# Matmuls of ones with the identity, read by nobody, ahead of thirteen steps of TensorE in the first two blocks

## The reference

```
first block:   h = rms_norm(x); proj = h @ w_in
               differential attention (4 heads x 2 maps) and block attention (8 heads), partial rope, gated by silu
               x = x + (sigmoid(g_a) * y_a + sigmoid(g_b) * y_b) @ w_out
               x = x + sigmoid(x @ w_ple_gate) * (p @ w_ple);  x = rms_norm(x)
second block:  mod = silu(c) @ w_mod + b_mod      (six vectors of 1024)
               h = rmsnorm(x) * (1 + sc1) + sh1;  proj = h @ w_in_2
               attention over compressed keys, selected blocks and a window, with a relative bias; short convolution
               x = x + gt1 * (concat(rmsnorm(o_attn), rmsnorm(o_conv)) @ w_out_2)
               h2 = rmsnorm(x) * (1 + sc2) + sh2
               x = x + gt2 * peer(h2)             (8 heads pick 16 of 16384 experts each)
out = rmsnorm(x)
```

## Time and profile before

| | |
|---|---|
| median of 3 runs | 1353.32 us (1350.22 to 1356.21) |
| profiled execution, its own time | 1355.46 us |
| its span, first to last instruction | 1353.7 us |
| mean granted clock of TensorE | 0.968 |
| TensorE matmul busy | 1251.1 us (92% of the span) |
| TensorE weight load busy | 1145.1 us (85%) |
| VectorE busy | 850.4 us (63%) |
| ScalarE busy | 711.5 us (53%) |
| POOL busy | 582.5 us (43%) |
| chain that ended last | PE 50%, POOL 21%, issue 14%, DVE 8%, ACT 4%, DMA 2% |

### The profile page before, as it was taken

The page is one execution under the profiler, slowest core; times in us unless marked ns, Lnnn a source line. Parts: engine busy times, 40 slices in busy tenths (PEclk is TensorE's granted clock), DMA queues, the critical chain, the costliest instruction groups (busy, mean ns, idle before and its releaser), DMA issues.

```text
span 1353.7 us, 26683 instructions
## 1 busy us (share of the span) xinstructions
PE 1251.1 (92%) x8546; PEld 1145.1 (85%) x8546; DVE 850.4 (63%) x1810; ACT 711.5 (53%) x1473; POOL 582.5 (43%) x500
## 2 busy tenths in 40 slices
PE   7979989977889888989899999999999999999996
PEld 6968878875877688989899999999978878888885
DVE  4596767877445553999645555553067767676765
ACT  5435757434545544645564444445555655555554
POOL 2563454432326632899986666667800000000000
PEclk8999999988899898999999999999999999999998
DMA  6575645674543333445455655565567675756552
GB/s 217 163 237 166 221 169 193 206 237 136 191 164 128 126 114 121 156 155 186 140 171 179 188 178 188 178 188 181 193 233 250 200 246 189 255 195 249 195 191 93
DMA packets 85471, 249.35 MB, mean 184 GB/s; under 512 B 7931, under 2 KB 29563, under 8 KB 84508
## 3 DMA queue, kind: packets, MB, share of 16 engines
q1 hardware_dynamic: 77212, 209.69, 47.0%
q0 software_dynamic: 8192, 38.80, 8.2%
HBM read 235.36 MB, written 13.11 MB: 184 GB/s over the span
## 4 chain that ended last, share of the span: by engine, by line
PE 50%; POOL 21%; issue 14%; DVE 8%; ACT 4%; DMA 2%; POOLq 1%; DVEq 0%; ACTq 0%; SPq 0%
PE psum L625 49%; POOL w_lo L1382 19%; DVE s_sb L1512 2%; POOL arena L1448 2%; DMA arena<-mods 1%; ACT w_hi L1048 1%; DVE w_lo L1503 1%; PE psum L788 1%; ACT arena L1185 1%; DVE arena L1732 1%; DMA s_sb<-routing_weights 1%; DVE rstd L1497 1%; POOLq L1381 0%; DVE arena L1618 0%; DMA par<-params 0%
## 5 line engine op out<-in xcount | busy, mean ns | idle before, releaser
L1048 ACT ACTIVATE w_hi<-ring 128x512 fp32r<-128x512 f32 x734 | 452.3, 629 | 416.2 <-PE psum L625 408.5
L1382 POOL TENSOR_TENSOR w_lo<-ring,w_hi 128x512 fp32r<-128x512 f32 x367 | 502.2, 1376 | 299.3 <-ACT w_hi L1048 292.1
L625 PE MATMUL psum<-h_hi,w_hi 128*128 128x256 f32 x1832 | 541.2, 295 | 53.3 <-DVE w_lo L1503 16.5
L625 PE MATMUL psum<-h_lo,w_hi 128*128 128x256 f32 x1832 | 524.7, 286 | 0.0
L625 PE MATMUL psum<-h_hi,w_lo 128*128 128x256 f32 x1832 | 523.9, 286 | 0.0
L625 PEld LDWEIGHTS psum<-h_hi,w_hi 128*128 128x128 f32 x1832 | 356.9, 195 | 73.1 <-issue 37.8
L625 PEld LDWEIGHTS psum<-h_lo,w_hi 128*128 128x128 f32 x1832 | 358.1, 195 | 0.3
L625 PEld LDWEIGHTS psum<-h_hi,w_lo 128*128 128x128 f32 x1832 | 357.4, 195 | 0.0
L1503 DVE TENSOR_TENSOR w_lo<-ring,w_hi 128x512 fp32r<-128x512 f32 x239 | 180.9, 757 | 140.9 <-ACT w_hi L1048 140.7
L625 PE MATMUL psum<-w_hi,h_hi 128*128 128x512 f32 (+1 forms) x592 | 225.1, 380 | 8.9 <-DVE arena L1520 5.4
L625 PE MATMUL psum<-w_hi,h_lo 128*128 128x512 f32 (+1 forms) x592 | 223.7, 378 | 0.0
(11 more groups left out here) (182 smaller groups left out, 1027.9 us busy)
## 6 DMA issues: line engine op xcount, KB each, us to landing
ring<-u_t SPq DMA_DIRECT2D x128, 512.0 KB, 3.5
ring<-v_rows SPq DMA_DIRECT2D x128, 512.0 KB, 3.5
ring<-weights SPq DMA_DIRECT2D x115, 512.0 KB, 4.1
arena<-mods POOLq DMA_DIRECT2D x48, 512.0 KB, 4.8
routing_weights<-s_sb SPq DMA_DIRECT2D x32, 320.0 KB, 4.2
s_sb<-routing_weights POOLq DMA_DIRECT2D x5, 2048.0 KB, 9.8
bias_rows<-arena POOLq DMA_DIRECT2D x1, 1536.0 KB, 5.9
xres<-x_t SPq DMA_DIRECT2D x1, 1024.0 KB, 4.8
```

What stands on the lines that cost most here:

```text
L625: return nc.tensor.matmul(out, lhs, rhs, start=start, stop=stop, **kw)
L1048: nc.scalar.activation(w_hi[:, half, :], src, ACT.Copy).then_inc(hi_done, 1)
L1382: nc.gpsimd.tensor_tensor(w_lo[:, half, :], src, w_hi[:, half, :].bitcast(F32), ALU.subtract)\
```

## The change

A new helper `fill_wait(count)` issues `count` matmuls of `ones` (128 by 128) with `ident` (128 by 128), f32, into the `a` buffer that is to be used next; nobody reads the result, and the next user of the buffer overwrites it. `take_a` notes the number of the buffer last taken. The helper waits for the constants and for the emptying of the buffer before the last one taken. It is called ahead of the steps' own waits, in thirteen places, with 120 matmuls in all: norm 2 (6), mv (14), nq0 (8), nq1 (14), turns 4, 7, 8, 9 and 15 (6, 4, 6, 9, 14), out2 (10), cmpt (10), mix 0 (5), wq (14).

```diff
@@ take_a
             def take_a(n):
+                nonlocal filled_a
+                filled_a = n
                 if n >= 2:
                     pe_.wait_ge(a_read, n - 1)
                 return abuf(n)
@@ new helper
+            filled_a = 0
+
+            def fill_wait(count):
+                if not count:
+                    return
+                n = filled_a + 1
+                pe_.wait_ge(const_set, 1)
+                pe_.wait_ge(small_in, 16 * 10)
+                pe_.wait_ge(a_read, n - 1)
+                for _ in range(count):
+                    mm(psum[:, n % 2, 0:P], ones[:, :], ident[:, :], True, True)
@@ norm
                     pe_.wait_ge(const_set, 1)
+                    if k == 2:
+                        fill_wait(6)
@@ proj in ROWS, ahead of pe_.wait_ge(h_ready, ...)
+                    if s[1] == "mv":
+                        fill_wait(14)
@@ proj
                     base = 0 if s[1] in FIRST1 + FILL1 else 8
+                    if s[1] in ("nq0", "nq1"):
+                        fill_wait(8 if s[1] == "nq0" else 14)
@@ turn
                     p = s[1]
+                    fill_wait({4: 6, 7: 4, 8: 6, 9: 9, 15: 14}.get(p, 0))
                     pe_.wait_ge(probs_done, p + 1)
@@ out1, out2
+                    if kind == "out2":
+                        fill_wait(10)
@@ mix
+                    if s[1] == 0:
+                        fill_wait(5)
```

## The result

The changed kernel took 1342.35 us in the median of 4 runs (1341.17 to 1342.95), the kernel before 1353.51 in 4 runs, the three known from above and one more (1350.22 to 1356.21): 0.9915 of it, with an interval of 0.9899 to 0.9931. That is 11.2 us less. The time is inside the range and 1.55 above the 1340.8 that was forecast. The profiled execution took 1341.17 us, 14.3 less than that of before, where 14.7 were forecast; but that one execution of before was 2.0 slower than its median.

A forecast was written before the change was run, and what follows sets the result against it. The prediction blamed stretches of TensorE at 1.2 GHz in place of 2.4, mostly behind waits. Its terms, less turn 7's loss, summed to 14.7 us, taken off the profiled 1355.5 for 1340.8; range 1335.5 to 1350.0.

The forecast's parts named there:

- mv: Fills in a 4.30 us wait ahead of mv: 5.65 us of low-clock work at full clock, 2.8 us gained.
- turn 4: Six fills in a 1.69 us wait: the 3.3 us of scores and projection behind it speed up, 1.7 us gained.
- turn 7: Four fills where TensorE had no wait: they delay ScalarE's queue and the PLE step, 0.9 us lost.
- norm 2: Six fills in a 2.07 us wait: the sums of squares go from 6.68 us to 3.5, 3.2 us gained.
- nq1: Fourteen fills in a 4.30 us wait: 4.46 us of busy low-clock work speeds up, 2.2 us gained.
- turn 9: Nine fills in a 2.48 us wait: worth 1.6 us for TensorE, but only 0.5 us counted as gained.
- turn 15, mix 0: Fills in waits of 4.14 and 1.30 us: turn 15 to 0.88 us, mix 0's sums to 1.9, 2.4 us gained.
- out2: Ten fills overrun a 0.89 us wait without loss; 2.8 us of busy low-clock work speeds up, 1.4 us gained.
- rival 2: Other engines' next waits take gains back; only mv, nq1 and out2 keep 6.4 us, less 0.9: 1350.0 us, chance 0.09.
- The skill's bound: The Trainium skill puts clock ramps under 1% of span, 13.5 us; the prediction's treated stretches gave 15.6, 1.15%.
- Rival 1: Too few fills in the small waits to hold the clock: 6.8 us of the sum lost, 1347.6 us, chance 0.18.
- From 545 us nothing but a shift: From 545 us on, the expert loops would only start earlier, with no other change in the profile.

The follow-up runs named there:

- first, second and third profile of the change: The changed kernel, then the same kernel unedited in two more sets of runs: 1342.35 us, then 1342.70 and 1343.18 us.
- The 33-row kernel: The changed kernel with its 120 fills made over 33 rows of ones and ident in place of 128: 1354.70 us, ratio 1.0004.
- the kernel without the useless fills: The changed kernel without the fills ahead of nq0, wq and turn 7, 26 of the 120: 1341.40 us, ratio 0.9920.

## Why the prediction was right, and where it was off

Measured by the marks, first, second and third profile of the change:

| term | forecast | measured |
|---|---|---|
| mv | 2.8 | 2.52, 2.50, 2.52 |
| turn 4 | 1.7 | 1.50, 1.48, 1.48 |
| turn 7 | -0.9 | about -0.9, -0.9, -0.6 |
| norm 2 | 3.2 | 2.11, 2.15, 0.47 |
| nq0 | 0 | 0 |
| nq1 | 2.2 | 1.97, 1.99, 1.96 |
| cmpt, turn 8 | 1.4 | 1.16, 1.16, 1.13 |
| turn 9 | 0.5 | 0.81, 0.82, 0.77 |
| turn 15, mix 0 | 2.4 | 1.42, 1.44, 1.43 |
| out2 | 1.4 | 0.98, 0.98, 0.99 |
| wq | 0 | 0.02 |
| sum | 14.7 | 11.6, 11.6, 10.2 |

(Turn 7 is the loss from turn 5 to turn 7 less the 0.26 that remains without its fills. Turn 15 with mix 0 is read from turn 15's own start, 464.59 in before, to pv 15, and norm 2 from bias 0 to nq0.)

- *The mechanism held, and is shown for three places.* At mv, nq1 and turn 15 the low stretch is gone in every profile with the full counts, ten of them, and stands there in every one without fills, with half of them or with 33 rows. mv gave 2.5 and turn 15 with mix 0 1.4 in all ten. Nearly half of TensorE's time in such a stretch comes back where it is on the path. These three make 5.9 of the 11.2; where the other 5.3 come from, place by place, isn't shown. The 33-row kernel takes the clock's answer away and leaves everything else, and its ratio is 1.0004: as a whole the gain is the clock's.
- *The sum was 3 us too high,* and the profiled execution hid it: of its 14.3, some 2.2 come from the gate and 1.5 from the expert stage. The medians are 11.2 apart, near the sum of the measured terms. That agreement is worth little, since turn 4 and turn 9, 2.3 of the sum, are there without fills too, and out2 not in every profile.
- *That the time came within 1.6 us was in part luck.* The gain of the medians was 3.5 less than forecast. But the forecast took it off the profiled execution, 2.0 above the median of before, and left those 2.0 in. Its reason, that the fills would level such differences, held in part at best: the runs of the change still spread over 4.4 and 5.7 us in its second and third set.
- *Norm 2 (3.2 forecast, 0.5 to 2.2)* is the term most mis-sized. The prediction took the low stretch from the sums of squares on the earlier trace rows, that is, behind the wait. But bias 0's 33-row matmuls run just ahead, the clock can fall in those, and then the six fills take 2.85 us in a wait of 2.07. The text had the 33-row case among its rows and didn't ask where it stood ahead of a wait. Where it did not fall there, in the kernel without the useless fills, the place gave 2.99: the price was right, and the condition missing. Without fills this place gave 1.3 in one profile, so their own share is open.
- *Turn 15 and mix 0 (2.4 forecast, 1.4).* Turn 15 gave its 0.7. TensorE did the sums of mix 0 at full speed, but it waited 0.18 and 0.65 us for ScalarE's squares (at 456.43 and 458.61), and they gave 0.75 of 1.7. With the clock up another engine set the pace: what rival 2 said, in this one place.
- *Half was too much.* mv, nq1, turn 4, turn 8 and out2 gave 70 to 90% of their forecasts. The prediction halved the busy time. The rows give the price of one matmul: 26 in 5.65 us before, 0.217 each, and 46 in 5.43 after, 0.118 each. 26 times the 0.099 between is 2.57, where mv gave 2.52; nq1's 21 in 4.46 us and 56 in 6.75 after make 1.93, and it gave 1.97. A stretch at low clock gives back 43 to 46% of its busy time here, not 50. At out2 the same count makes 1.2, and 1.0 was measured; the rest is open. Turn 9 was 0.3 too low, if its 0.8 is the fills' at all.
- *The signs that it named.* The waits left ahead of mv, nq1, turn 15 and wq are 1.27, 1.18, 1.02 and 1.06, the clock is 0.990 and there are 240 records more, as said. The sums of norm 2 took 4.05 us in the first profile, not 3.5. Of the ten treated stretches, one is at 0.50 in the first and third profiles (norm 2) and two in the second (norm 2 and wq), where none or one was allowed.
- *Turn 7 was right in place and size:* 0.6 to 0.9 late by the marks, and passed to PLE through ScalarE in full. The medians don't show it.
- *The skill's bound.* By it the ramps together are worth under 13.5 us. What was measured doesn't contradict it: those treated gave 11.2 us, 0.83% of the median, where the prediction had them at over 1%. What all of them cost together no run shows, since low stretches were left in every kernel.
- *Rival 1 (the small waits give nothing)* did not come true, by the medians, but its opposite, that each small fill holds its own stretch, isn't shown either: turns 4 and 9 were clear in every later profile, those without their fills too, and wq and out2 were not always clear with them. What the rival rested on was sound for the 33-row matmuls and wrong for transposes.
- *"From 545 us nothing but a shift" was wrong.* The treated stretches shift the expert stage by 12.75, 14.20 and 9.20 us in the three profiles, and by the end the lead is 14.28, 12.54 and 9.36: +1.5, -1.7, +0.2. Nothing treated lies there; why this stage differs from one execution to the next was not tested. Such differences are as large as any one term, which is why only the marks show the terms.

## What to carry to other kernels

Where the profile shows TensorE at half its clock behind a wait of several us, matmuls over all 128 rows that nobody reads, placed in that wait, can be worth nearly half of the busy time that follows, but only of the part that nothing else paces. Count them to fit: too few in a long wait leave the gap that brings the fall, and any where TensorE isn't waiting are paid for in full, or double if the clock is already down. Price each one by itself with marks in the trace, since a median can't tell terms of 1 us, and take more than one profile, of the kernel before too, before calling a stretch that comes and goes a gain.

## What was unexpected of the hardware

- Matmuls over 33 rows, at the same duration (3.39 us for 14, against 3.29), did not keep the clock: 1.0004 against 0.9918 on the same chip, and 16.9 us at 0.50 with TensorE busy for 16.85 of them.
- f32 transposes over 128 rows kept it as well as matmuls did: 0.9923.
- A fill met at low clock took 0.45 to 0.8 us in place of 0.23, and the dearer ones were those between 33-row matmuls.
- The low stretch at the gate, in a step that the change doesn't touch, was 6.8 us long in before, 3.4 in the change's first two profiles and 6.9 in its third, and with ten fills ahead of it absent in two kernels and 3.3 in a third.
- The same wait of 1.94 us inside out2 had a fall of the clock behind it in two profiles (0.51 and 0.52 in the stretch) and none in the change's (1.00).
